# A hybrid attention and DeltaNet block: new order of SyncE's transfers and VectorE's rounds, and GpSimd's weight remainder in two operations

## The reference

```python
h = rmsnorm(x, pre_norm_gain) * (1.0 + scale[:, None, :]) + shift[:, None, :]
proj = h @ w_in
...
o_a = dsa_attention(qa, ka, va, q_idx, k_idx, iw)      # the 128 best keys of each query, by an index score
y_a = (o_a * jax.nn.silu(az)) @ w_a_out
...
o_b = gated_delta_rule_chunked(qb, kb, vb, g, beta)    # needs inv(I + lower) of each chunk
y_b = (rmsnorm(o_b, dn_norm_gain) * jax.nn.silu(bz)) @ w_b_out
y = jax.nn.sigmoid(ga) * y_a + jax.nn.sigmoid(gb) * y_b
return x + gate[:, None, :] * rmsnorm(y @ w_o, post_norm_gain)
```

## Time and profile before

| | us |
|---|---|
| median of three runs | 861.46 (860.87 to 861.50) |
| the profiled execution, its own time | 862.66 |
| its span, first to last instruction | 860.9 |
| TensorE busy | 812.2 (94%) |
| VectorE busy | 460.7 (54%) |
| ScalarE busy | 332.3 (39%) |
| GpSimd busy | 364.9 (42%) |

### The profile page before, as it was taken

How to read it: one execution, slowest core, us unless ns; L and a number is a source line. 1 busy time by engine, 2 the same in 40 slices (tenths; PEclk the granted TensorE clock), 3 DMA queues, 4 the chain that set the end, 5 groups by cost and what they waited for, 6 DMA issues and landing times.

```text
span 860.9 us, 11101 instructions
## 1 busy us (share of the span) xinstructions
PE 812.2 (94%) x4070; PEld 651.9 (76%) x4070; DVE 460.7 (54%) x953; ACT 332.3 (39%) x702; POOL 364.9 (42%) x226
## 2 busy tenths in 40 slices
PE   6989968999999879999999999999999999999997
PEld 2467745777877768888888777777777788878897
DVE  5268585795778796576566435443544333232113
ACT  1357623634434243543542543343334322212231
POOL 0233731353525334454445434434443444533541
PEclk9999987999999999999999999999999999999999
DMA  8927744244333423332322222223222353552602
GB/s 314 341 67 247 211 120 95 63 108 110 99 87 88 72 67 90 100 86 75 93 67 74 74 70 76 58 66 97 74 69 58 95 171 123 173 160 83 194 28 98
DMA packets 165648, 95.62 MB, mean 111 GB/s; under 512 B 34881, under 2 KB 158146, under 8 KB 164058
## 3 DMA queue, kind: packets, MB, share of 16 engines
q1 hardware_dynamic: 165594, 94.91, 38.2%
HBM read 85.11 MB, written 9.22 MB: 110 GB/s over the span
## 4 chain that ended last, share of the span: by engine, by line
PE 70%; DVE 15%; DMA 5%; ACT 4%; SPq 2%; issue 2%; POOL 0%; DVEq 0%; POOLq 0%; ACTq 0%
PE ps L675 16%; PE ps L677 16%; PE ps L676 16%; PE ps L945 2%; PE ps L785 2%; DVE yq L1687 2%; DVE binv L1745 2%; PE ps L996 2%; PE ps L995 2%; PE ps L994 2%; PE ps L932 2%; DMA w_ada_sb<-in_w_ada 2%; DVE kraw L1687 2%; PE ps L714 2%; ACT prob L1249 2%
## 5 line engine op out<-in xcount | busy, mean ns | idle before, releaser
L1345 POOL TENSOR_TENSOR w_lo<-raw,w_hi 128x1024 fp32r<-128x1024 f32 (+1 forms) x109 | 263.0, 2418 | 368.3 <-ACT w_hi L1018 352.1
L675 PE MATMUL ps<-h_hi,w_hi 128*128 128x512 f32 (+1 forms) x680 | 290.9, 428 | 3.0 <-ACT xT L1040 1.1
L677 PE MATMUL ps<-h_hi,w_lo 128*128 128x512 f32 (+1 forms) x680 | 268.0, 394 | 0.0
L676 PE MATMUL ps<-h_lo,w_hi 128*128 128x512 f32 (+1 forms) x680 | 266.9, 393 | 0.0
L675 PEld LDWEIGHTS ps<-h_hi,w_hi 128*128 128x128 f32 (+1 forms) x680 | 128.6, 189 | 30.1 <-issue 4.8
L677 PEld LDWEIGHTS ps<-h_hi,w_lo 128*128 128x128 f32 (+1 forms) x680 | 128.3, 189 | 29.1
L676 PEld LDWEIGHTS ps<-h_lo,w_hi 128*128 128x128 f32 (+1 forms) x680 | 128.9, 189 | 24.8 <-issue 3.4
L1018 ACT ACTIVATE w_hi<-raw 128x1024 fp32r<-128x1024 f32 (+1 forms) x109 | 113.6, 1051 | 25.9 <-PE ps L996 17.1
L1189 ACT ACTIVATE o_tok<-ps 128x128 f32<-128x128 f32 x32 | 8.9, 277 | 108.6 <-PE ps L897 108.4
L995 PE MATMUL ps<-w_lo,y_hi 128*128 128x256 f32 x128 | 36.2, 283 | 0.0
L996 PE MATMUL ps<-w_hi,y_lo 128*128 128x256 f32 x128 | 36.2, 283 | 0.0
(11 more groups left out here) (271 smaller groups left out, 1383.9 us busy)
## 6 DMA issues: line engine op xcount, KB each, us to landing
raw<-in_w_in SPq DMA_DIRECT2D x84, 512.0 KB, 3.7
w_ada_sb<-in_w_ada SPq DMA_DIRECT2D x8, 1024.0 KB, 12.7
inverse_tiles<-zero SPq DMA_DIRECT2D x4, 1032.0 KB, 5.4
raw<-in_w_b_out SPq DMA_DIRECT2D x8, 512.0 KB, 3.8
raw<-in_w_a_out SPq DMA_DIRECT2D x8, 512.0 KB, 3.8
ada<-in_w_ada SPq DMA_DIRECT2D x8, 512.0 KB, 4.7
raw<-in_w_o SPq DMA_DIRECT2D x8, 512.0 KB, 3.8
x_sb<-in_x SPq DMA_DIRECT2D x4, 512.0 KB, 11.9
```

The costliest lines, as they stand in the source:

```text
L675: pe.matmul(out_ap, w_hi[:, slot, k, 0:m], rhs_hi(k), start=(k == 0), stop=False)
L676: pe.matmul(out_ap, w_hi[:, slot, k, 0:m], rhs_lo(k), start=False, stop=False)
L677: mm = pe.matmul(out_ap, w_lo[:, slot, k, 0:m], rhs_hi(k), start=False, stop=(k == KT - 1))
L1345: pool.tensor_tensor(w_lo[:, slot, :, 0:n], raw[:, slot, :, 0:n], w_hi[:, slot, :, 0:n].bitcast(F32), ALU.subtract).then_inc(lo_made, 1)
```

## The change

The unit list gets the keys of head 6 before the first DeltaNet head (in place of the fourth merge gate) and those of head 7 in the place of head 6. The Gram groups, the two inversions, the key rows of the index branch (now round 20), the zeroing, the decay rows and the block loads move to other rounds; head 7's key taps and the query and value taps are cut over two rounds; the first logit of each group of six waits for its own pair of returned rows. GpSimd forms the remainder of a unit in two operations of 512 columns.

```diff
...
-         + [("K", h) for h in range(4, 6)]
-         + [("GA", n) for n in range(4)])
-for _h, _extra in enumerate((("K", 6), ("K", 7), ("GA", 4), ("GA", 5), ("GA", 6), ("GA", 7), ("AQ", 0), ("AK", 0))):
+         + [("K", h) for h in range(4, 7)]
+         + [("GA", n) for n in range(3)])
+for _h, _extra in enumerate((("K", 7), ("GA", 3), ("GA", 4), ("GA", 5), ("GA", 6), ("GA", 7), ("AQ", 0), ("AK", 0))):
...
-R_LOW = [10, 11, 13, 14, 17, 18, 46, 50]
-R_GRAM = [13, 15, 17, 19, R_DELTA[0] + 2, R_DELTA[0] + 6, R_DELTA[1] + 6, R_DELTA[2] + 6]
-R_INV = [24, 97]
-INV_ROWS = [(1, 2), (3, 4, 5), (6, 7), (8, 9), (10, 11), (12,), (13,), (14,), (15,)]
-R_PAIR = [[38 + 2 * n for n in range(8)], [R_INV[1] + 12 + n for n in range(8)]]
+R_LOW = [10, 11, 12, 13, 30, 33, 46, 50]
+R_GRAM = [12, 13, 14, 17, R_DELTA[0] + 1, R_DELTA[0] + 4, R_DELTA[0] + 7, R_DELTA[1] + 6]
+R_INV = [24, R_DELTA[1] + 12]
+INV_ROWS = [[(1, 2, 3), (4, 5), (6, 7), (8, 9), (10, 11), (12,), (13,), (14,), (15,)],
+            [(1, 2), (3, 4), (5,), (6,), (7, 8), (9,), (10,), (11,), (12,), (13,), (14,), (15,)]]
+R_STORE = [R_INV[b] + len(INV_ROWS[b]) for b in range(2)]
+R_PAIR = [[42, 44, 45, 47, 49, 50, 52, 53], [R_DELTA[2] + n for n in (12, 14, 16, 18, 20, 24, 26, 27)]]
...
-R_TURN = ends_at("I", 3) + 3
-R_LOGIT = [R_TURN + 7 + 14 * m // 23 for m in range(24)]
+R_TURN = ends_at("I", 3) + 2
+R_LOGIT = [R_TURN + 8 + 14 * m // 23 for m in range(24)]
...
-    zero = place("zero", [P, 4 * NT * (P // SUB) * (SUB * P + SUB) // P], at=where["th"] + 3 * ROW)
+    zero = place("zero", [P, 4 * NT * (P // SUB) * (SUB * P + SUB) // (3 * P)], at=where["U"])
...
-    s_turned, s_back, s_kodd = sem("index_rows_gathered"), sem("index_rows_returned"), sem("odd_key_rows_loaded")
+    s_turned, s_kodd = sem("index_rows_gathered"), sem("odd_key_rows_loaded")
+    s_back = [sem(f"index_rows_returned{n}") for n in range(4)]
...
-                sp.dma_start(inv_dram[n].rearrange("(p f) -> p f", p=P), zero[:]).then_inc(s_zero, 16)
+                for part in range(3):
+                    sp.dma_start(inv_dram[n].rearrange("(a p f) -> a p f", a=3, p=P)[part], zero[:]).then_inc(s_zero, 16)
...
             if h == 4:
-                sp.wait_ge(*inv_dve.at(f"r{SUB - 1}", 0))
+                sp.wait_ge(*pair_dve.at("r7", 0))
...
-            sp.wait_ge(s_zero, 2 * 16 if b == 0 else 4 * 16)
+            sp.wait_ge(s_zero, 6 * 16 if b == 0 else 12 * 16)
...
-        def load_pairs(b):
+        def load_corners(b):
...
+        def load_pairs(b):
...
+            if h == 0:
+                sp.wait_ge(s_zero, 12 * 16)
...
-                    sp.dma_start(iq[64 * b:64 * b + 16, n, :], isw[32 * n + 16 * b:32 * n + 16 * b + 16, 0, :]).then_inc(s_back, 16)
+                    sp.dma_start(iq[64 * b:64 * b + 16, n, :], isw[32 * n + 16 * b:32 * n + 16 * b + 16, 0, :]).then_inc(s_back[n], 16)
...
-            if r == 0:
-                clear((0, 1))
-            if r in (20, 26):
-                clear((2,) if r == 20 else (3,))
...
-                for h in range(HEADS):
+            if r in (8, 24, 36):
+                for h in {8: range(4), 24: (4, 5), 36: (6, 7)}[r]:
...
-            if r == 11:
+            if r == 22:
...
-                if r == R_GRAM[h] + 4:
-                    lower_blocks(h)
...
-                if r == R_INV[b] + len(INV_ROWS):
+                if r == R_GRAM[4 * b + 3] + 3:
+                    for h in range(4 * b, 4 * b + 4):
+                        lower_blocks(h)
+                if r == R_STORE[b] - 4:
+                    load_corners(b)
+                if r == R_STORE[b]:
...
-                if r == R_PAIR[b][0] - 2:
+                if r == R_STORE[b] + 2:
...
+            if r in (22, 26, 40, 43):
+                clear(((22, 26, 40, 43).index(r),))
...
-                    mm = pe.transpose(ps[:, 5, blk(i)], kdup[:, i, :], ident)
+                    mm = pe.transpose(ps[:, 3, blk(i)], kdup[:, i, :], ident)
...
-                    pe.wait_ge(s_back, 8 * 16)
+                if m % 6 == 0:
+                    pe.wait_ge(s_back[m // 6], 2 * 16)
...
-            if h == 0:
-                pe.wait_ge(*small_dve.at("kx"))
-            elif h >= 2:
-                pe.wait_ge(*gram_dve.at("L", h - 2 if h < 5 else h - 1))
+            if h >= 2:
+                pe.wait_ge(*gram_dve.at("L", h - 2 if h < 4 else h - 1))
             if h >= 4:
-                pe.wait_ge(*solve_act.at("kd", max(0, h - 5)))
+                pe.wait_ge(*solve_act.at("kd", h // 7))
...
+                if h == 0:
+                    pe.wait_ge(*small_dve.at("kx"))
...
-                if h <= 2:
-                    pe.wait_ge(*gram_dve.at("L", h + 5))
+                if h <= 1:
+                    pe.wait_ge(*gram_dve.at("L", h + 6))
...
-            elif r == 9:
+            elif r == 20:
...
-                if m == 0:
-                    act.wait_ge(s_zero, 4 * 16)
...
-                if h >= 6:
-                    act.wait_ge(*z_dve.at("s", h - 6))
+                if h == 7:
+                    act.wait_ge(*z_dve.at("s", 0))
...
-                act.wait_ge(*key_dve.at("s", 5 if h == 0 else 6 if h == 1 else 7))
+                act.wait_ge(*key_dve.at("s", 6 if h == 0 else 7))
...
+                    act.wait_ge(*pair_dve.at("r7", 0))
...
-            elif rel == len(INV_ROWS):
+            elif rel == len(INV_ROWS[b]):
...
-            pool.tensor_tensor(w_lo[:, slot, :, 0:n], raw[:, slot, :, 0:n], w_hi[:, slot, :, 0:n].bitcast(F32),
-                               ALU.subtract).then_inc(lo_made, 1)
+            for ks in (slice(0, KT // 2), slice(KT // 2, KT)):
+                ins = pool.tensor_tensor(w_lo[:, slot, ks, 0:n], raw[:, slot, ks, 0:n], w_hi[:, slot, ks, 0:n].bitcast(F32),
+                                         ALU.subtract)
+            ins.then_inc(lo_made, 1)
...
-            elif r == 9:
+            elif r == 20:
...
-                dve.tensor_scalar(kx[:], bank(5), pcol[:, 1, R2_LNG:R2_LNG + 1], pcol[:, 1, R2_LNB:R2_LNB + 1], ALU.mult,
+                dve.tensor_scalar(kx[:], bank(3), pcol[:, 1, R2_LNG:R2_LNG + 1], pcol[:, 1, R2_LNB:R2_LNB + 1], ALU.mult,
...
-            pairs = {2: (0, 0), 6: (0, 1), 9: (0, 2), 10: (1, 0), 12: (1, 1), 15: (1, 2)}
+            pairs = {1: (0, 0), 3: (0, 1), 6: (0, 2), 10: (1, 0), 12: (1, 1), 15: (1, 2)}
...
-        def taps(made, acts, y, src, j, h):
-            for n in (1, 2, 3):
+        def taps(made, acts, y, src, j, h, ns=(1, 2, 3)):
+            for n in ns:
...
-            if rel == 0:
+            if h < 7 and rel == 0:
...
+            elif h == 7 and rel in (0, 1):
+                taps(key_dve, key_act, kraw[:, h, :], bank(unit_bank("K", h)), 1, h, ((1,), (2, 3))[rel])
...
-            if rel == 4:
-                taps(q_dve, q_act, yq[:], bank(unit_bank("Q", h)), 0, h)
+            if rel in (4, 5):
+                taps(q_dve, q_act, yq[:], bank(unit_bank("Q", h)), 0, h, ((1,), (2, 3))[rel - 4])
...
-            elif rel == 8:
-                taps(v_dve, v_act, yv[:], bank(unit_bank("V", h)), 2, h)
+            elif rel in (8, 9):
+                taps(v_dve, v_act, yv[:], bank(unit_bank("V", h)), 2, h, ((1,), (2, 3))[rel - 8])
...
-            if h == 4:
-                dve.wait_ge(*pair_dve.at("r7", 0))
...
-            if 0 <= rel < len(INV_ROWS):
-                for i in INV_ROWS[rel]:
+            if 0 <= rel < len(INV_ROWS[b]):
+                for i in INV_ROWS[b][rel]:
...
-            prod = diag[:].rearrange("p i f -> p (i f)").rearrange("p (i c j) -> p i c j", i=4, c=SUB // 2)
+            prod = binv[:, 0:2].rearrange("p a i j -> p (a i j)").rearrange("p (i c j) -> p i c j", i=4, c=SUB // 2)
...
-                dve.wait_ge(*gram_dve.at(f"ss{NT - 1}", 4 * b + 3))
+                dve.wait_ge(s_inv[b], 2 * 16)
...
+                    dve.wait_ge(*pair_dve.at("r7", 1))
```

## The result

The changed kernel takes 851.72 us (median of four executions, 849.76 to 852.48) against 861.48 us; the ratio is 0.9884, 95% interval 0.9867 to 0.9902. It is faster by 1.2%, as forecast in direction, and 6.7 us slower than the 845.0 forecast, inside the range of 837 to 855. The profiled execution took 849.76 us (span 848.0), 12.9 less than that of before, where the sum said 16.2.

The account below looks back on a forecast made before the run. It took TensorE as the bound, with one large wait of 11.8 us for the first index logit's returned rows. 8.8 + 2.85 + 0.8 - 7.0 + 10.8 = 16.2 us saved from 862.66, less 1.2 to the median: 845 us, range 837 to 855.

Parts of the forecast that it names:

- Part 1: Round 38: the first index logit's wait falls from 11.84 to 3 us, saving 8.8, plus 2.85 of lost clock.
- I take it that so short a wait leaves the clock up: Round 38: a wait of 3 us brings no half clock, so 2.85 us are saved.
- the changed order puts as much in front of it: Ahead of the last gather: zeroing, decay rows and weight loads as before; issue at 108.55, landing about 114.5 us.
- Part 2: Round 6: zeroing a third of `zero` removes TensorE's 0.8 us wait for the decay; 0.8 us saved.
- Part 3: Rounds 52 to 63: a later last corner step delays `U`, with waits for `L` and another Gram group; 7.0 us lost.
- Part 4: Rounds 64 to 127: inversion rows and corners spread over rounds 80 to 111; 10.8 us saved.
- Rival A: VectorE doesn't keep up in rounds 80 to 111: Part 4 saves 3 instead of 10.8; 853 us, chance 0.20.
- Part 5: GpSimd's remainder in two operations: costs nothing, and no gain counted apart from the VectorE waits within Part 4.
- the signs I had named for being right: Logit wait under 4 us, PEclk 1.00 around round 38, `U` wait 4 to 7, period 33.7, long VectorE products gone.
- B: Rival: Part 3 costs only 3, the logit doesn't wait (Part 1 saves 14), Part 4 saves 12.5; 837 us, chance 0.17.
- C: Rival: full transfer engines hold the returning rows, wait stays 8 us with half clock, Part 1 saves 3.8; 853, chance 0.08.
- D: Rival: slower, VectorE holds GpSimd's second half and `w_lo` comes late at TensorE; 874 us, chance 0.02.

Follow-up runs that it names:

- the changed kernel again: The changed kernel, unedited, run again on the chip of three follow-up kernels: 849.91 us, ratio 0.9861 to the kernel before.
- the one-operation kernel: The changed kernel with GpSimd's remainder again in one operation of 1024 columns: 854.08 us, ratio 0.9907 to the kernel before.
- the three moves: The changed kernel with ScalarE's first decay behind K3's tap, six zero transfers in rounds 0 and 1, and first-inversion corners in rounds 40 to 50: 841.84 us.
- the kernel with late corners on top: The three moves with the first and third corner steps of the second inversion one round later (97 and 101): 840.61 us.

## Why the prediction was right in direction and 6.7 us too low

- **Part 1, the wait at round 38: the stage saved 6.7 in place of 11.65.** TensorE is busy for 36.5 us in rounds 38 to 51 before and after, so nothing of the 2.85 us for the clock was saved: "I take it that so short a wait leaves the clock up" failed, and 6.8 us at half clock lie around the 4.2 us wait. The wait for the rows is 1.2 longer than the forecast 3, and 1.0 is a wait for the ReLU that had no term. These three make up the 5.0 that are missing.
- **Behind the wait, a step that failed and was hidden by luck.** "Next late are the gathered rows" held, and so did the rotation's 7 us and the two transfers in place of eight. But "the changed order puts as much in front of it" counted bytes and not issues: SyncE issues twenty transfers from the last store to the last gather where it issued seven. I had the gather issued at 108.55 as before and landed at about 114.5; it was issued at 111.56 and VectorE had it at 117.79, the rotation ended at 124.83 in place of 121, and the rows were back at 127.57 in place of 123.5 to 124.4. TensorE's arrival I had at 120.7, and it was 123.40, for the rounds 12 to 19 that I gave no cost. Two things late by some 3 us left the wait between them near the forecast; when TensorE alone came on time, it was 8.3 us. Behind SyncE's issues stands ScalarE's copy behind the inversion (the ReLU's 3.4 us when the rows came earlier).
- **Rounds 12 to 19: a step left out, +3.1.** I moved the Gram groups forward and the decays with them, and counted the two rounds gained but not what ScalarE's row holds. The decay's wait for its row stands in front of a tap; one round later for it takes the wait away (18.9 to 15.0). So the last `L` came 0.5 us earlier than before (97.70 against 98.16) and not 2.7, and the inversion's start at 103.37 is only just inside the forecast 101 to 103.5.
- **Part 2** came as forecast in the first profile (round 6 is 0.8 us shorter) and by half in that of the changed kernel again, where 0.4 us of the wait for the decay is left.
- **Part 3, +7.0: right in mechanism, mis-sized, +9.4.** The waits came to what I had added: 3.8 for `U` in place of 6 and 3.1 for the Gram in place of 1.3, 5.0 more than before where I had 5.4. What was mis-sized is the rest: TensorE is busy for 4.4 us more than before where I had 1.6, and two stretches of 3.4 us at half clock lie in it (the clock of 0.91). `U` itself landed 23.5 us behind the start of round 52, forecast 22.4; the wait for it was short because TensorE was late as well. The corners moved forward alone take 5 us out of these rounds.
- **Part 4, -10.8: measured -14.3,** and -12.4 in the profile of the changed kernel again. By quarters of 16 rounds it is 34.2, 35.0, 35.3 and 32.8 us where I had 35.7, 34.8, 36.6 and 33.7. VectorE did not keep up better than I had it: against the new normal period of 32.8 the rounds 80 to 111 are 4.7 us too long, against 33.6 I had added 4.2. Rival A is wrong, and the difference to the forecast is about the 0.83 us of each of the four heads that the cut taps give.
- **The taps cut over two rounds: no term at all.** The waits for `resid` of 5.7 us in seven pieces were the sign of it; I called a normal period 33.62 and never asked what stood in it. The 2.5 us of three periods, the 1.0 of round 197, which is the split's, and 0.3 in rounds 176 to 191 are the -3.8 from round 128 on.
- **Part 5, the split at zero: wrong by 3.5 to 4 us.** "Elsewhere TensorE is the bound and it gives nothing" fails in round 197, by 1.0 us. For rounds 12 to 127 I folded it into the 3 and 1.2 us of part 4 without a figure of its own, and the rest lies there, as far as single profiles tell. I had seen that a wait lasts until GpSimd's operation ends, and did not sum it: 27 us of VectorE's busy time. Nor was it free for GpSimd: two halves take 2.76 us in the mean where one operation took 2.43, so 0.3 a unit and not 0 to 0.2.

So the unpriced losses (3.1, the clock) and the unpriced gains (taps, split) nearly cancelled, and the closeness owes a part to that. Of the signs I had named for being right, the clock of 1.00 around round 38 did not come (0.76 and 0.95), and the waits at the logit (4.2) and for `U` (3.8) lie just outside their bounds; the long VectorE products are gone (1.8 us at most), and the period came out shorter (32.8 for 33.7). Rivals B and C fall: the logit waits, but not 8 us, and part 3 does not come cheap. D's hold exists and costs nothing to see at TensorE, whose wait for `w_lo` is 1.0 us here and was 0.8. What stays open: why the one-operation kernel's own profile, its fastest execution of six, shows only 1.3 us of the 4 in rounds 12 to 19 (the wait for `L` is 3.9 in place of 2.6) and 1.3 from 128 on, with less time in between, why a wait of the same length is followed by half clock in one execution and not in another, and where the 0.4 us in rounds 176 to 191 come from that differ between executions of the same kernel.

## What to carry to other kernels

When a wait is taken away, write down what each in-order queue has in front of the next arrival, the engine that only issues transfers included: here the first logits were held in turn by SyncE's issues and by ScalarE's copy, neither of which the sum had priced. Price every operation that stands unbroken in front of a short result that the bound engine wants; cutting it so that the result slips in between was worth 0.8% here, more than any other single edit of these experiments. A wait of the matrix engine costs itself and often some microseconds of half clock behind it, so a wait made half as long is not half the cost, and the forecast wants a range for it.

## What the runs showed of the hardware that I had not expected

- Waits of 2.6 us (round 14), 4.2 us (round 38) and 3.1 and 3.8 us (rounds 56 and 59) of TensorE were each followed by 3.4 or 6.8 us at 1.2 GHz; around the wait of 11.8 us before it was 13.9 (9.9 and 4.0, by the earlier trace rows). It isn't certain to follow: behind the same wait of 3.3 us for the ReLU it was 3.4 us with the three moves and nothing in the kernel with late corners on top.
- SyncE spent 15.1 us in issuing 22 transfers (97.72 to 113.36, less some gaps), and the last gather was the last two of them. One zero transfer took between 0.43 and 1.39 us to issue.
- VectorE's 953 instructions took 27 us less with GpSimd's operations cut in half, and a wait that ends with GpSimd's operation is what they lost: 2.43 us for `ob_lo` against 1.35.
